# The low parts of all dense weights are subtracted on GpSimd in place of VectorE

## The reference

```python
def decoder_layer(x, c, ...):
    mod = (silu(c) @ w_ada + b_ada).reshape(B, 3, 3, D_MODEL)
    x = sub_out(x, swiglu(sub_in(x, 0), ffn_up[0], ffn_down[0]), 0, 0.5)
    h = sub_in(x, 1)
    pa, pb, pg = split_cols(h @ w_in, [A_COLS, B_COLS, 2 * D_MODEL])
    ya, ... = rwkv7_branch(pa, ...)
    yb, ... = gdn_branch(pb, ...)
    g_a, g_b = split(sigmoid(pg), 2)
    x = sub_out(x, (g_a * ya + g_b * yb) @ w_out, 1, 1.0)
    x = sub_out(x, swiglu(sub_in(x, 2), ffn_up[1], ffn_down[1]), 2, 0.5)
```

## Time and profile before

| | |
|---|---|
| runs of the kernel before | 2300.72, 2300.95, 2302.95 us; median 2300.95 |
| the profiled execution, its own time | 2309.99 us |
| its span in the profile | 2308.3 us |
| TensorE busy | 2076.7 us, 90%, granted clock 0.915 on average |
| VectorE busy | 1269.5 us, 55% |
| ScalarE busy | 958.1 us, 42% |
| GpSimd busy | 4.8 us, 0% |
| weights and the rest, from memory | 332 MB read, 152 GB/s over the span |

### The profile page before, as it was taken

One profiled execution on the slowest core, in us unless ns is written; L12 is line 12 of the kernel. 1 busy time (PEld: TensorE's weight loads), 2 busy tenths in 40 slices (PEclk: granted clock), 3 DMA queues, 4 the chain that ended last, 5 costly groups with the idle time before them and its releaser, 6 DMA issues.

```text
span 2308.3 us, 44992 instructions
## 1 busy us (share of the span) xinstructions
PE 2076.7 (90%) x19116; PEld 1863.6 (81%) x19116; DVE 1269.5 (55%) x2227; ACT 958.1 (42%) x1890; POOL 4.8 (0%) x30
## 2 busy tenths in 40 slices
PE   6999898989989896899989998988798988779997
PEld 4899777878878875788989996877797877569997
DVE  3454445654466256577556644464554744658863
ACT  3343553434475304423454445333345642153343
POOL 0000000000000000000000000000000000000000
PEclk7999999989999867899999999889899987689999
DMA  7877555555555615587646664444344444237863
GB/s 244 227 223 209 153 168 164 147 143 142 145 140 148 159 46 128 151 240 228 192 124 181 177 176 135 119 122 111 89 117 125 110 116 121 71 101 211 231 195 95
DMA packets 593718, 353.35 MB, mean 153 GB/s; under 512 B 57140, under 2 KB 554326, under 8 KB 591966
## 3 DMA queue, kind: packets, MB, share of 16 engines
q1 hardware_dynamic: 489344, 302.23, 45.9%
q10 hardware_dynamic: 104174, 48.25, 8.7%
HBM read 332.27 MB, written 18.50 MB: 152 GB/s over the span
## 4 chain that ended last, share of the span: by engine, by line
PE 73%; DVE 9%; DMA 6%; ACT 5%; ACTq 4%; issue 3%; SPq 0%; DVEq 0%
PE bank L858 70%; DMA ring<-in_w_ada 3%; ACTq L620 2%; DVE ring_r L726 1%; DMA ring<-in_ffn_up 1%; PE bank L639 1%; ACT w_hi_r L718 1%; DVE big L1838 1%; DVE far L1838 1%; PE bank L652 1%; DMA far<-t_blocks 1%; DVE y L1841 1%; DVE h L1838 1%; DVE y L1838 1%; PE bank L647 1%
## 5 line engine op out<-in xcount | busy, mean ns | idle before, releaser
L858 PE MATMUL bank<-big_r,w_hi_r 128*128 128x264 f32 x4160 | 1091.4, 297 | 49.7 <-DVE h_r L1838 37.6
L858 PE MATMUL bank<-big_r,ring_r 128*128 128x264 f32 (+1 forms) x3456 | 1004.1, 291 | 0.0
L858 PEld LDWEIGHTS bank<-big_r,w_hi_r 128*128 128x128 f32 x4160 | 758.1, 194 | 126.8 <-issue 94.9
L858 PE MATMUL bank<-h_r,w_hi_r 128*128 128x264 f32 x2752 | 807.7, 293 | 0.0
L726 DVE TENSOR_TENSOR ring_r<-ring,w_hi_r 128x1024 fp32r<-128x1024 f32 (+2 forms) x440 | 524.2, 1195 | 464.9 <-ACT w_hi_r L718 461.2
L858 PEld LDWEIGHTS bank<-big_r,ring_r 128*128 128x128 f32 (+1 forms) x3456 | 673.7, 195 | 1.0
L718 ACT CAST w_hi_r<-ring 128x1024 fp32r<-128x1024 f32 (+2 forms) x440 | 452.8, 1030 | 480.5 <-PE bank L858 291.7
L858 PEld LDWEIGHTS bank<-h_r,w_hi_r 128*128 128x128 f32 x2752 | 541.4, 197 | 1.1
L858 PE MATMUL bank<-big,far 64*64 64x64 f32 (+2 forms) x1440 | 159.1, 266 | 0.0
L858 PEld LDWEIGHTS bank<-big,far 64*64 64x64 f32 (+1 forms) x1440 | 124.5, 144 | 7.6 <-issue 7.1
L858 PE MATMUL bank<-ring,c 128*32 128x256 f32 x1152 | 96.4, 415 | 20.9 <-DMA ring<-in_w_ada 15.6
(11 more groups left out here) (288 smaller groups left out, 1981.5 us busy)
## 6 DMA issues: line engine op xcount, KB each, us to landing
ring<-in_ffn_up SPq DMA_DIRECT2D x176, 512.0 KB, 4.3
ring<-in_w_in SPq DMA_DIRECT2D x148, 512.0 KB, 3.8
ring<-in_w_ada SPq DMA_DIRECT2D x144, 512.0 KB, 4.1
ring<-in_ffn_down SPq DMA_DIRECT2D x64, 512.0 KB, 3.8
far<-in_state_gdn_ssm ACTq DMA_DIRECT2D x28, 512.0 KB, 5.4
ring<-in_ffn_down SPq DMA_DIRECT2D x32, 384.0 KB, 3.2
ring<-in_w_out SPq DMA_DIRECT2D x16, 512.0 KB, 3.8
out_sample_gdn_ssm<-far ACTq DMA_DIRECT2D x16, 512.0 KB, 4.2
```

The source lines that it names most:

```text
L858: return pe.matmul(out, lhsT, rhs, start=start, stop=stop)
```

## The change

`low` is called for GpSimd. Its calls leave VectorE's queue in all places, and a block for GpSimd in each layer makes them in the same order of m, one after another, each behind its own wait for `hi_ready`. What is subtracted, where it is written and what signals it are as before. Loads, ScalarE's copies and TensorE's matmuls keep their order.

```diff
-        def low(dve, m):
+        def low(pool, m):
...
-            dve.wait_ge(hi_ready.sem, hi_ready.nth(m + 1))
+            pool.wait_ge(hi_ready.sem, hi_ready.nth(m + 1))
             w = ring[:, slot[n], 0:size]
-            dve.tensor_tensor(ring_r[:, slot[n], 0:size], w, w_hi[:, m % HI, 0:size].bitcast(F32), ALU.subtract).then_inc(lo_ready.sem, lo_ready.one())
+            pool.tensor_tensor(ring_r[:, slot[n], 0:size], w, w_hi[:, m % HI, 0:size].bitcast(F32), ALU.subtract).then_inc(lo_ready.sem, lo_ready.one())
...
+                @block.gpsimd
+                def _(pool):
+                    first = split_no[(l, "up0", 0)]
+                    last = split_no[(l + 1, "up0", 0)] if l + 1 < DEPTH else len(splits)
+                    for m in range(first, last):
+                        low(pool, m)
+
...
-                            for g in range(2):
-                                ahead(dve, low, (l, f"up{i_ffn}", 2 * t + g))
...
-                        for n in range(3 * NT):
-                            ahead(dve, low, (l, f"down{i_ffn}", n))
...
-                    for m in range(0 if l else 2):
-                        low(dve, m)
...
-                        ahead(dve, low, (l, kind, i))
...
-                    for o in range(NT):
-                        ahead(dve, low, (l, "out", o))
```

## The result

The changed kernel takes 2440.03 us (median of 4 runs, 2433.0 to 2446.81) against 2301.95 us before (4 runs, 2300.72 to 2304.33): ratio 1.060, 95% interval 1.057 to 1.063. It is slower, and above the predicted range of 2299 to 2380. The profiled execution took 2439.4 us with a span of 2437.6, so 129.3 us more span than the one shown before.

A forecast was written before the change was run, and what follows sets the result against it. TensorE, busy 90% of the span, was taken as the bound, VectorE having room on average. Late tiles 10, exclusion 24, second up stage 5, solve -3 gave +36 us on 2300.95: 2337 us, range 2299 to 2380.

The forecast's parts named there:

- GpSimd's price: One 1024-element subtraction on GpSimd: 2.3 us against VectorE's 1.23, so +1.07 us; bounds 1.0 and 3.1 us.
- The fear of 2.93 us: Rival, feed-forward stages: above 2.93 us an operation GpSimd becomes the bound, 2385 us and more; chance 0.14.
- Late tiles: Tiles where TensorE starts right behind the subtraction, mostly where loads are late: lose 12.5 us, part returns, +10 us.
- Other feed-forward tiles at 0: All other feed-forward tiles: 2.5 to 3.3 us of slack hide the extra 1.07 us, cost 0.
- the second up stage of layer 1: Up stage of the second feed-forward: VectorE's state updates and GpSimd's subtractions take turns, +5 us in layer 1.
- The gain in the solve turns: Turns 67 and 68: the solve no longer stands behind a subtraction, 1.5 us gained per layer, 3 us.
- Two engines side by side: Preparation turns: VectorE's two-operand products and GpSimd's subtraction exclude each other, 2.0 us in 12 turns, +24 us; chance 0.58.
- The hint of the earlier trace: First microseconds: a 32x8 copy takes 0.25 us beside a GpSimd fill, 0.15 alone; taken as a hint of exclusion.
- The exclusion's own range: Forecast case in which VectorE's products and GpSimd's subtraction exclude each other: 2315 to 2365 us, chance 0.58.

The follow-up runs named there:

- e8: The changed kernel with each GpSimd subtraction made as two halves of 512 elements; 2436.05 us, ratio 1.057 to the kernel before.
- e3: The kernel before plus four GpSimd subtractions of 128x256, read by nobody, beside each tile of the mixing stages; 2466.02 us, ratio 1.070.
- e4: The kernel before plus eight GpSimd fills of 128x256, read by nobody, beside each tile of the mixing stages; 2307.85 us, ratio 1.000.
- e5: The changed kernel, with GpSimd's subtraction waiting in each preparation turn until VectorE's products are done; 2329.41 us, ratio 1.010 to the kernel before.
- e6: The kernel before, GpSimd unused, with seven unread VectorE products ahead of the turn's own in each preparation turn; 2445.47 us, ratio 1.062.
- e7: The kernel before with VectorE's subtraction placed behind the products in the 8 preparation turns, likewise in turns 66 and 67; 2298.73 us, ratio 0.997.

## Why the prediction was wrong

**GpSimd's price** was right: 2.3 us predicted, 2.39 median (row above: mean 2.41). The fear of 2.93 us did not come true. Its make-up was in part luck. The medians of 1024, 768 and (in e8) 512 elements are 2.39, 1.84 and 1.29 us, which is 2.15 ns an element and 0.2 us besides; the forecast took 2 x 0.84 ns an element from the selects and made up the difference by counting the fixed part of a select twice and adding 0.2 us.

**Late tiles** came near: TensorE's wait for ring_r rose from 5.4 to 13.5 us (some 15 expected), though only 7.4 of these lie in the first feed-forward block, where nearly all was expected. **Other feed-forward tiles at 0** was right too in the sense of slack, but not for the feed-forward stages as a whole: they lose 24 us, where late tiles (10) and the second up stage of layer 1 (5) gave 15. That up stage lost 6.0 (5 expected): 3.8 of it are longer waits, 2.8 for big_r at its end and 1.0 for ring_r, and 2.2 a lower clock. What I had left out is the fp32r cast and low part of the hidden activations in every up turn, both blocked. In the first up stage of layer 0, VectorE's timeline of the changed kernel has, beside the pair of subtractions of GpSimd that begins at 51.16:
```profile
53.37 0.43 DVE L1845 TENSOR_TENSOR big<-big,bank 128x264 f32<-128x264 f32 x1 [4.15 <-PE bank L858]
53.84 2.24 DVE L1933 CAST big_r<-big 128x264 fp32r<-128x264 f32 x1
56.11 0.43 DVE L1845 TENSOR_TENSOR big_r<-big,big_r 128x264 fp32r<-128x264 f32 x1
```
TensorE waits for big_r once at the end of each of the four up stages, and these waits rose by 8.4 us in sum. As 2.8 of them are in the 6.0 us just told, 5.6 go towards the missing 9; the rest isn't divided, and nothing tested it by itself.

**The gain in the solve turns** (3 us) did not come. The subtraction is out of VectorE's queue, but it comes back through GpSimd. The chain of the changed kernel in the second half of the solve in layer 0, where the earlier trace rows had the subtraction and then, by the same view, steps of 0.18 to 0.23 us (the rows name it turn 67, but the solve begins there and its second half, to which they belong, is turn 68):
```profile
799.16 2.36 DVE big L599
801.52 0.02 issue
801.54 0.22 DVE big L600
...
802.01 2.26 DVE big L600
```
Two links of the chain wait for one subtraction each: 4.2 us lost where 1.2 were freed. By the first matmuls of their tiles, turns 66 to 70 take 32.3 us in place of 31.2, and 32.6 in place of 31.3 in layer 1.

**Two engines side by side** is the step that failed: "So 0.84 to 3.1 us a turn; nothing says who wins the gap, so I take the middle, 2.0 us: 12 x 2.0 = +24 us". The mechanism was right and is shown (e3, e4, e5), and so, nearly, was the count of 12 turns (TensorE waits in 14, and in 12 of the 16 by 2.1 us or more longer). The cost of a turn, 2.8 us on average, lay within the bounds. The hint of the earlier trace rows was no evidence for it: that was a copy beside a fill, and e4 shows that fills don't stretch these products. Two things make most of the way from +24 to +107. The cost per turn lies near the upper bound, not in the middle: 2.8 us in place of 2.0, so 12 x 2.8 = 34. And I put a us of waiting at one us; the clock behind a wait is a term that the sum puts at nothing without saying so. What follows the waits is a stretch at the 1.2 GHz level: 59 us more in the two mixing stages, and e6 shows the same kind of multiple, 137 for 48 of standing still, without GpSimd. The other 16 us of standing still (above) are in the sum as -3 for the solve turns and nothing else. The rows for it were at hand: in the kernel before, the turn before that of the earlier trace rows waits 2.6 us for the products, and the windows behind it read
```profile
1447.00:1453.20 6.20, 3.60 (x30) 1.00 0.64 191
1453.20:1457.00 3.80, 3.79 (x28) 0.61 0.14 41
1457.00:1461.00 4.00, 4.00 (x40) 0.50 0.00 0
1461.00:1466.00 5.00, 5.00 (x36) 0.50 0.12 17
```
I read the waits and never the clock behind them. With 34 in place of 24 and 59 for the clock, the forecast's own sum would give 2301 + 10 + 34 + 59 + 5 - 3 = 2406, above its range already. With 16 for the rest of standing still in place of the -3, and the 9 us of the feed-forward stages, it is 2434 of the 2440 measured.

The chances: slower had 0.78 and came. The exclusion's own range of 2315 to 2365 had bounds from the wait's size alone, so no case in it could reach 2440.

## What to carry to other kernels

Work is not free because it goes to an idle engine: ask what VectorE executes while it runs. A GpSimd operation that reads SBUF stops a VectorE operation with two SBUF inputs until it ends, and the moved subtraction does so to the fp32r cast too; then one gets through and the next is stopped, so a chain of many short products is the worst neighbour; where it must be, let GpSimd wait for the end of the chain (e5: 16 waits, 111 us).

Price a wait on TensorE with the clock behind it. Before adding up waits, take the windows behind the longest ones that are there already: if they stand at 0.50, the new wait may cost two to three times its length, as it did here (109 us for 50 of standing still in the change, 137 for 48 in e6). That shortening a wait gives back as much is not shown: e7 took 7.1 us off the waits for the products and gained 7.6.

When the bound from above of an unknown cost comes from "the other slips in between", and the other is released by a steady upstream (ScalarE's copies here), assume that it does each time.

## What the runs showed of the hardware that was not expected

- The fp32r cast of 264 elements, with one SBUF input, is blocked beside GpSimd's subtraction as the two-input operations are: 298 ns before, 1071 on average in the change, 2.24 us in the row above.
- So is a one-input operation with a number for its second operand, the solve's 128x256 `tensor_scalar` (L593): 0.38 us before, up to 2.0 us beside GpSimd's subtraction, 0.92 us beside the reading operations of e3, and 0.38 us beside the fills of e4. These are few: three in e3, two in the change.
- One operation of VectorE passes between two of GpSimd, whether these take 2.4 or 1.34 us, and halving them gains nothing clear of the noise (ratio 1.057 against 1.060).
- Work of 3.2 us put on VectorE ahead of TensorE in each of 16 places, without any other change, cost 137 us: 48 of standing still and 89 of a lower clock (0.82 and 0.80 in the two stages, 0.89 and 0.86 before).
- GpSimd's operation in halves costs more in sum: 880 operations of 1.34 us are 1152.7 us busy, 440 of 2.41 are 1056.4.
